# Weight units of a transformer kernel in two halves: transfer, rounding, subtraction and the wait of TensorE

## The reference

```python
def sandwich_ffn(x, w_gate_up, w_down, g_pre, g_post, shift, scale, gate):
    h = modulate(rms_norm(x, g_pre), shift, scale)
    return x + 0.5 * gate * rms_norm(swiglu(h, w_gate_up, w_down), g_post)
...
for l in range(DEPTH):
    mx = [m[:, None, :] for m in mod_vectors(c, w_mod[l], b_mod[l])]
    mc = mod_vectors(c_ctx, w_mod[l], b_mod[l])
    x, ctx = sandwich_ffn(...), sandwich_ffn(...)
    out_x, out_c = token_mix(hx, hc, w_in[l], w_out[l], ...)
    x, ctx = sandwich_ffn(...), sandwich_ffn(...)
x = x + dilated_attention_mixer(...); x = x + swiglu_2(...)
x = x + mlstm_mixer(...);             x = x + swiglu_2(...)
```

## Time and profile before

| what | before |
|---|---|
| median of 3 executions | 2496.54 us (2496.41 to 2496.72) |
| the profiled execution | 2497.18 us, span 2495.4 us |
| PE matmuls busy | 2412.9 us, 97% |
| DVE busy | 1613.3 us, 65% |
| ACT busy | 1021.2 us, 41% |
| POOL busy | 338.9 us, 14% |
| mean granted clock of PE | 0.992 |
| transfers | 385.93 MB, mean 155 GB/s |

### The profile page before, as it was taken

One profiled execution on the slowest core, in us unless ns is written; L12 is line 12 of the kernel. 1 busy time (PEld: TensorE's weight loads), 2 busy tenths in 40 slices (PEclk: granted clock), 3 DMA queues, 4 the chain that ended last, 5 costly groups with the idle time before them and its releaser, 6 DMA issues.

```text
span 2495.4 us, 29343 instructions
## 1 busy us (share of the span) xinstructions
PE 2412.9 (97%) x12118; PEld 2004.8 (80%) x12118; DVE 1613.3 (65%) x2208; ACT 1021.2 (41%) x1431; POOL 338.9 (14%) x226
## 2 busy tenths in 40 slices
PE   7999989999999999999999989999999999999998
PEld 5887878857888778888888758887888888887987
DVE  7778686374778787543385466756566576586674
ACT  4221325365312225322225464445555544465443
POOL 0334252200143252101030200000000000000000
PEclk9999999999999999999999999999999999999999
DMA  8555552511555553544362615555544355443554
GB/s 284 185 171 184 171 173 96 156 34 57 164 174 181 164 174 120 165 138 152 103 219 92 148 52 193 186 186 163 184 128 159 118 193 190 153 142 119 187 186 142
DMA packets 242629, 385.93 MB, mean 155 GB/s; under 512 B 10880, under 2 KB 150400, under 8 KB 242432
## 3 DMA queue, kind: packets, MB, share of 16 engines
q1 hardware_dynamic: 236320, 372.43, 45.5%
q0 software_dynamic: 6176, 11.64, 2.4%
HBM read 382.83 MB, written 3.11 MB: 155 GB/s over the span
## 4 chain that ended last, share of the span: by engine, by line
PE 67%; DVE 17%; DMA 9%; ACT 4%; issue 3%; POOL 0%; DVEq 0%; SPq 0%; ACTq 0%
PE ps L542 17%; PE ps L544 16%; PE ps L543 16%; PE ps L548 8%; DVE arena L1906 8%; DMA raw<-in_w_mod 6%; PE ps L549 4%; DVE wlo L1883 3%; ACT whi L1255 2%; DVE arena L1903 1%; PE ps L617 1%; PE ps L876 1%; DMA grow<-gcol 1%; DMA raw<-in_w_ffn_gate_up 1%; PE ps L852 0%
## 5 line engine op out<-in xcount | busy, mean ns | idle before, releaser
L1255 ACT ACTIVATE whi<-raw 128x2048 fp32r<-128x2048 f32 x279 | 532.9, 1910 | 1122.3 <-PE ps L544 492.7
L1883 DVE TENSOR_TENSOR wlo<-raw,whi 128x2048 fp32r<-128x2048 f32 x279 | 663.3, 2378 | 489.3 <-ACT whi L1255 489.0
L542 PE MATMUL ps<-wlo,Hcut 128*128 128x512 f32 (+1 forms) x1888 | 706.2, 374 | 21.4 <-DVE Hcut L2087 13.1
L544 PE MATMUL ps<-whi,Hcut 128*128 128x512 f32 (+1 forms) x1888 | 695.9, 369 | 0.0
L543 PE MATMUL ps<-whi,Hcut 128*128 128x512 f32 (+1 forms) x1888 | 695.4, 368 | 0.0
L542 PEld LDWEIGHTS ps<-wlo,Hcut 128*128 128x128 f32 x1888 | 357.1, 189 | 89.3 <-DVE Hcut L2087 15.4
L544 PEld LDWEIGHTS ps<-whi,Hcut 128*128 128x128 f32 x1888 | 356.9, 189 | 59.8
L543 PEld LDWEIGHTS ps<-whi,Hcut 128*128 128x128 f32 x1888 | 357.4, 189 | 56.3
L542 PE MATMUL ps<-Hcut,whi 128*128 128x512 f32 (+1 forms) x1032 | 395.2, 383 | 4.9 <-DVE wlo L1883 4.9
L544 PE MATMUL ps<-Hcut,whi 128*128 128x512 f32 (+1 forms) x1032 | 394.6, 382 | 0.0
L543 PE MATMUL ps<-Hcut,wlo 128*128 128x512 f32 (+1 forms) x1032 | 394.4, 382 | 0.0
(11 more groups left out here) (269 smaller groups left out, 1806.9 us busy)
## 6 DMA issues: line engine op xcount, KB each, us to landing
raw<-in_w_ffn_gate_up SPq DMA_DIRECT2D x88, 1024.0 KB, 5.1
raw<-in_w_mod SPq DMA_DIRECT2D x65, 1024.0 KB, 5.2
raw<-in_w_ffn_down SPq DMA_DIRECT2D x44, 1024.0 KB, 4.9
raw<-in_ffn_w_in SPq DMA_DIRECT2D x44, 1024.0 KB, 5.1
raw<-in_attn_w_in SPq DMA_DIRECT2D x36, 1024.0 KB, 5.1
raw<-in_ffn_w_out SPq DMA_DIRECT2D x22, 1024.0 KB, 4.9
raw<-in_w_in SPq DMA_DIRECT2D x16, 1024.0 KB, 5.1
raw<-in_mlstm_w_in SPq DMA_DIRECT2D x12, 1024.0 KB, 5.1
```

Of the source, the lines that this page charges most:

```text
L542: e.matmul(o, L[0], R[1], start=start, stop=False)
L544: return e.matmul(o, L[0], R[0], start=False, stop=stop)
L1255: e.activation(hi_of(n), slot(n), ACT.Copy).then_inc(*A.up(("hi", n)))
L1883: e.tensor_tensor(lo_of(n), slot(n), hi_of(n).bitcast(F32), ALU.subtract).then_inc(*V.up(("lo", n)))
```

## The change

Every unit from the eighth on is handled in two halves, split along k: `half_of(n, h)` is the first or the second 1024 columns of a slot, which are k/2 row blocks.

- SP issues two transfers of 512 KB for a unit, each with a semaphore of its own. The first half is issued when the first half of the unit before it in the slot is done, if that was a side unit or a cut unit of the same k and m; otherwise, as before, when all of it is done. The second half is issued when all of it is done.
- ACT makes two roundings of 128x1024 in place of one of 128x2048, each after its own half has landed. DVE makes two subtractions, each after its own rounding.
- PE waits for the first half when it begins a unit and for the second when it comes to row block k/2 (`rows`).
- `side_sum` waits for the second half ahead of its fifth operation, and gives the first half back after its fourth.

No product, sum or order of the work on an engine is changed. The diff, cut to its core:

```diff
-        raw_landed = [Steps(sem(f"raw_landed{i}"), 16) for i in range(RAW)]
+        raw_landed = [[Steps(sem(f"raw_landed{i}_{h}"), 16) for h in range(2)] for i in range(RAW)]
...
+        def half_of(n, h):
+            k, m = units[n][1:3]
+            return slice(k // 2 * m * h, k // 2 * m * (h + 1))
...
-                w.wait_ge(*V.at(("lo", n)))
+                w.wait_ge(*V.at(("lo", n, 0)))
...
+            def rows(n, k):
+
+                if k == units[n][1] // 2:
+                    w.wait_ge(*V.at(("lo", n, 1)))
...
                     for k in range(8):
+                        rows(n, k)
...
-                        w.wait_ge(*landed(n).at(n))
                         if nth[n] >= CUT:
                             w.wait_ge(*T.at(("unit", cuts[nth[n] - CUT])))
-                        e.activation(hi_of(n), slot(n), ACT.Copy).then_inc(*A.up(("hi", n)))
+                        for h in range(2):
+                            z = half_of(n, h)
+                            w.wait_ge(*landed(n, h).at(n))
+                            e.activation(hi_of(n)[:, z], slot(n)[:, z], ACT.Copy).then_inc(*A.up(("hi", n, h)))
...
-                        w.wait_ge(*A.at(("hi", n)))
-                        e.tensor_tensor(lo_of(n), slot(n), hi_of(n).bitcast(F32), ALU.subtract).then_inc(
-                            *V.up(("lo", n)))
+                        for h in range(2):
+                            z = half_of(n, h)
+                            w.wait_ge(*A.at(("hi", n, h)))
+                            e.tensor_tensor(lo_of(n)[:, z], slot(n)[:, z], hi_of(n)[:, z].bitcast(F32),
+                                            ALU.subtract).then_inc(*V.up(("lo", n, h)))
...
-                w.wait_ge(*landed(n).at(n))
                 for k in range(4):
+                    if k % 2 == 0:
+                        w.wait_ge(*landed(n, k // 2).at(n))
...
-                        if (k, s) != (3, ns - 1):
+                        if (k, s) == (1, ns - 1):
+                            i.then_inc(*V.up(name, ("took", n, 0)))
+                        elif (k, s) != (3, ns - 1):
...
-                e.dma_start(kslot(n), units[n][0]).then_inc(*landed(n).up(n))
+                p, half = n - RAW, units[n][1] // 2
+                if n < FIRST:
+                    e.dma_start(kslot(n), units[n][0]).then_inc(*landed(n, 0).up(n))
+                    return
+                for h in range(2):
+                    if p >= FIRST:
+                        if kind_of[p] == "cut":
+                            w.wait_ge(*V.at(("lo", p, h if units[p][1:3] == units[n][1:3] else 1)))
+                        elif kind_of[p] == "side":
+                            w.wait_ge(*V.at(("took", p, h)))
+                        else:
+                            w.wait_ge(*T.at(("unit", p)))
+                    e.dma_start(kslot(n)[:, half * h:half * h + half, :], units[n][0][:, half * h:half * h + half, :]).then_inc(
+                        *landed(n, h).up(n))
```

More of the change, by code:

```diff
@@ L348, in build @@
             "row", "col", "out")}
-        every = [T, A, V, G, *first_landed, *raw_landed, *LD.values()]
+        every = [T, A, V, G, *first_landed, *[s for pair in raw_landed for s in pair], *LD.values()]
         def at(off, *dims):
@@ L488, in lo_of, with landed @@
             return wlo[nth[n] % CUT][:, 0:k * m]
-        def landed(n):
-            return first_landed[n] if n < FIRST else raw_landed[(n - FIRST) % RAW]
+        def half_of(n, h):
+            k, m = units[n][1:3]
+            return slice(k // 2 * m * h, k // 2 * m * (h + 1))
+        def landed(n, h):
+            return first_landed[n] if n < FIRST else raw_landed[(n - FIRST) % RAW][h]
         bank_of = {}
@@ L505, in mods_there @@
             if i < 2 and Q == "F00":
-                w.wait_ge(*V.at(("took", 4)))
+                w.wait_ge(*V.at(("took", 4, 1)))
         def pairs(l):
@@ L735, in out_product, with products @@
                 bs = {(t, h): bank(("y", P, t, h)) for t in range(nt) for h in range(2)}
-                def products(k, t, unit_of):
+                def products(k, t, n, unit_of):
                     L, (hi, lo) = left(k, t), unit_of
+                    rows(n, k % 2)
                     for h in range(2):
@@ L748, in out_product @@
                         for t in range(nt):
-                            i = products(k, t, parts)
+                            i = products(k, t, n, parts)
                         i.then_inc(*T.up(("k", P, k), *[("unit", n)] if k % 2 else []))
@@ L788, in project_tile @@
                         n, (hi, lo) = unit(4, 512, kt // 4 - (feed.count - first_unit[0]))
+                    rows(n, kt % 4)
                     ready(Q, t, kt, b)
@@ L2807, in fetch @@
             def fetch(n):
-                if n >= FIRST + RAW:
-                    p = n - RAW
-                    if kind_of[p] == "cut":
-                        w.wait_ge(*V.at(("lo", p)))
-                    elif kind_of[p] == "side":
-                        w.wait_ge(*V.at(("took", p)))
-                    else:
-                        w.wait_ge(*T.at(("unit", p)))
-                e.dma_start(kslot(n), units[n][0]).then_inc(*landed(n).up(n))
+                p, half = n - RAW, units[n][1] // 2
[12 more added lines that the diff above has]
+                        *landed(n, h).up(n))
             e.dma_start(vec[:, :], a["vec"]).then_inc(*LD["vec"].up("vec"))
```

12 lines of the change are left out of this document (6 added, 6 removed).

## The result

| | before | after |
|---|---|---|
| median, us | 2496.63 (2496.41 to 2499.87, 4 runs) | 2479.37 (2478.18 to 2480.05, 4 runs) |
| profiled execution, us | 2497.2 | 2480.05 |
| its span, us | 2495.4 | 2478.2 |

The ratio is 0.9926, 95% interval 0.9914 to 0.9938: 17.3 us less. In a later session, with more runs, it came out the same: 2476.95 against 2494.13 us, ratio 0.993 (0.9918 to 0.9943).

The account below looks back on a forecast made before the run. PE was taken as the bound, with matmuls in flight for 97% of 2495.4 us. Terms -13.1 - 7.8 - 2.1 + 3.0 = -20.0 us took the profiled 2497.2 to 2477.2, median 2476.5, range 2471 to 2491.

Parts of the forecast that it names:

- Landings and early slots: Down products: earlier first halves of `w_mod` remove DVE's landing idles and PE's six waits for the activation's low part, -13.1 us.
- with 6.2 us less behind it DVE reaches L2087 at 342.0: First layer's down product: without four landing idles DVE makes the low part before PE wants it at 345.8.
- giving slots back earlier: Side units: next first half issued about 2.7 us earlier; said to count where DVE is busy 82.88 of 95 us.
- First half of a subtraction: Cut units: PE starts after half a rounding and half a subtraction, removing waits of 7.3 and 0.5 us, -7.8 us.
- Restarts: PE: each of 13 waits that go gives 0.16 us more than its recorded idle time, -2.1 us.
- Added instructions: DVE and ACT: extra work of 20 and 39 us, mostly beside PE's products; +3.0 us on the path, 0 to 5.3.
- 3 us of range: Low end: DVE held some 1 us less per wait for a rounding could shorten softmax and norm chains at three places.
- PE's second wait: PE: 279 more waits cost nothing where the semaphore is already there, 0 us.
- the first rival: Down products: DVE stays the bound through work, the six waits stay, gain 5.9 us, 2490.6 us; chance 0.13.
- Slower through halves as long as wholes: Layers of 256 tokens: a pair of halves lands in 10.2 us, PE loses 30 us, about 2530 us; chance 0.04.
- The early halves' condition: Slots: the shape condition and SP's in-order waits make early first halves rare, landings stay, 2493 us; chance 0.08.

Follow-up runs that it names:

- e4: The change, but both halves of every slot are given back only when all of it is done; transfers still in halves: 2478.57 us, ratio 0.9937.
- e10: The kernel before, with POOL's twelve bias transfers of layer two issued ahead of its additions: 2492.26 us, ratio 0.9992.
- e3: The kernel before with rounding and subtraction in halves, PE waiting for both at a unit's start, transfers and slots whole: 2486.23 us, ratio 0.9964.
- e5: The kernel before with only transfers split, side sums starting on the first half; slots given back whole, computing whole: 2484.13 us, ratio 0.9963.
- e2: The kernel before with rounding, subtraction and PE's wait in halves; transfers and slots whole: 2485.08 us, ratio 0.9964.
- e9: The change again without an edit, run beside the kernel before: 2476.95 us, ratio 0.9930.
- e12: The change with a second reduction, a maximum that changes no value, behind each of POOL's 56 sums: 2494.40 us, ratio 1.0004 to the kernel before.

## Why the prediction was right, and where it was not

It said 2476.5 us, 2471 to 2491, faster; it is 2479.4. The direction, the places in the down products and the price of the added work were right; the sum came out near by errors that cancel. Step by step:

- **Landings and early slots, -13.1 for the low part.** The right place and sign. Measured: 9.9 us in the table of matmuls (3.4, 1.7, 3.2, 1.6), and 3.5 us of waits stay. The transfer was sized well enough (3.9 us taken, 4.0 to 4.8 found). The step that failed is "with 6.2 us less behind it DVE reaches L2087 at 342.0": idle time of DVE was counted as time it could work in, though POOL was at work there and slows it. DVE did reach it at 340.77 in place of 348.25, but 4.1 us of that it had at the stretch's start, 286.66 for 290.77: 3.4 of the 6.2 us were won. Nor is "giving slots back earlier" what counts most: e4 does without it and is 1.2 us from the change.
- **First half of a subtraction, -7.8.** The waits went, as said, 5.5 us of them at 220, 244 and 842 us, with 1.7 from the clock on top (the one at 842 is missing in e10's trace too). The reason was wrong: e3 and e5 lose most of them with PE waiting for whole units, and PE's early start has only the 1.2 us between e2 and e3 for it. They went when DVE was less late, by either relief.
- **Restarts, -2.1.** Not to be told apart; the matmul at 349.07 gained 3.37 us for a stall of 3.28.
- **Added instructions, +3.0.** The wrong sign, the worst of the four. The prices were right: two halves of a subtraction take 2.35 us for 2.29 (0.07 was taken), DVE does 27 us more for the 20 forecast, ACT 29 for 39. But the other effect of the same edit, DVE starting under ACT's second half, was waved off with 3 us of range; e3 has the two together at 8.4 us gained, an error of 11.4 us. The Trainium skill's fixed cost per tile ("VectorE: DVE Perf Modes", the section on the TRN2 errata), which the prediction weighed and set aside, would have made this term larger still. For two operations back to back the row of 2.35 us speaks against it.
- **PE's second wait, 0.** Right: 34.00 of 34.00 us.
- **Not foreseen:** 5.7 us in the mLSTM layer with 0.9 from the clock, which is the larger part of what e3 gains; 3.7 us lost at the bias load (0.5 in e9's trace); 1.5 us lost at the start of the run, where the clock was lower and the first landing came 0.66 us later.
- **The rivals.** The down products kept two of six waits, so the first rival had a third of the truth: DVE is busy all through that stretch. Slower through halves as long as wholes: a half does take 4.0 to 4.8 us, but the two of a pair run side by side, 5.14 us for both. Going against the rule to batch to 1 MiB, from "DMA: Bandwidth & Descriptors" (section Bandwidth) of the Trainium skill, cost nothing here: e5, which only splits transfers, is 10.0 us faster than before. The early halves' condition was met often: in the change only 65 pairs of transfers go out within 1 us of each other, in e5 342. It would have mattered little (e4).

The errors were 3 to 11 us each and of both signs. That the total came within 3 us of the forecast is luck to that extent.

## What to carry to other kernels

When several engines are late by one account, test each relief alone: the parts here are worth 8 to 13 us each and 17 together, and the one booked as a cost was a gain. Splitting a unit in two pays first where one engine can start while the engine before it does the second half, and where work can start on the half that has landed; handing buffers back by halves may add little. Before idle time of DVE is counted as room, look at what POOL does in it. And read a stall of 1 or 2 us in a single trace with a second trace of the same kernel beside it.

## What the runs showed of the hardware

- A reduction over partitions on POOL holds DVE: an operation of 0.48 us took 2.47, and 56 more reductions made DVE busy 42 us longer.
- A load of 512 KB takes 4.0 to 4.8 us where 1 MB takes 5.1, and two issued 0.41 us apart are both there after 5.14; with twelve bias transfers of 128 KB under way it takes 15.4.
- A stall of PE of some 2 us at 244 us was followed by a granted clock of 0.72 over six microseconds; without the stall it stayed at 1.00. A stall of 3.28 us at 349 us was followed by no drop; one of 3.08 us in e12 was followed by 0.52 from 343 to 350 us.
